# Three norms of a two-block transformer kernel: squares added over pairs of features by VectorE ahead of one ones product

## The reference, cut to what matters

```
def rmsnorm(x, g):
    x32 = x.astype(jnp.float32)
    y = x32 * lax.rsqrt(jnp.mean(x32 * x32, axis=-1, keepdims=True) + EPS)
    return (y * g.astype(jnp.float32)).astype(x.dtype)
```

## Time and profile before

| | us |
|---|---|
| median of 3 runs | 1694.67 |
| lowest, highest | 1693.54, 1696.02 |
| profiled execution | 1695.31 |
| its span, first to last instruction | 1693.1 |
| PE busy | 1655.0 (98%) |
| DVE busy | 1168.1 (69%) |
| ACT busy | 922.9 (55%) |
| POOL busy | 756.2 (45%) |

### The profile page before, as it was taken

One profiled execution on the slowest core, in us unless ns is written; L12 is line 12 of the kernel. 1 busy time (PEld: TensorE's weight loads), 2 busy tenths in 40 slices (PEclk: granted clock), 3 DMA queues, 4 the chain that ended last, 5 costly groups with the idle time before them and its releaser, 6 DMA issues.

```text
span 1693.1 us, 31046 instructions
## 1 busy us (share of the span) xinstructions
PE 1655.0 (98%) x10698; PEld 1467.9 (87%) x10698; DVE 1168.1 (69%) x2092; ACT 922.9 (55%) x1515; POOL 756.2 (45%) x357
## 2 busy tenths in 40 slices
PE   8999999999999999999999999999999999999998
PEld 8778999988999998888888879968899988789997
DVE  4772289777777777788777876365755579675555
ACT  4573455587666665545455464265555564555554
POOL 4500668888999991000000004403455744235553
PEclk9999999999999999999999999999999999999999
DMA  6303555587555547888888863303555543146553
GB/s 248 99 27 120 168 201 184 185 284 264 180 178 168 181 165 256 287 287 290 291 291 288 289 232 100 98 2 125 174 186 185 184 149 117 62 153 187 186 185 123
DMA packets 86343, 312.38 MB, mean 184 GB/s; under 512 B 9843, under 2 KB 9843, under 8 KB 86131
## 3 DMA queue, kind: packets, MB, share of 16 engines
q1 hardware_dynamic: 85972, 309.38, 54.5%
q0 software_dynamic: 288, 1.97, 0.3%
HBM read 310.26 MB, written 1.05 MB: 184 GB/s over the span
## 4 chain that ended last, share of the span: by engine, by line
PE 84%; DVE 7%; ACT 3%; issue 3%; POOL 1%; DMA 1%; DVEq 0%; SPq 0%; ACTq 0%; POOLq 0%
PE psr L898 17%; PE psr L838 15%; PE psr L1154 10%; PE acc_all L1154 10%; PE psr L901 9%; PE acc_all L838 7%; PE psr L1101 3%; PE psr L1046 2%; PE psr L785 1%; DVE arena L2561 1%; POOL wl L571 1%; DVE wl L571 1%; ACT wh L562 1%; PE psr L933 1%; PE psr L826 1%
## 5 line engine op out<-in xcount | busy, mean ns | idle before, releaser
L571 POOL TENSOR_TENSOR wl<-ring,wh 128x1024 fp32r<-128x1024 f32 x276 | 674.2, 2445 | 556.9 <-ACT wh L562 541.5
L562 ACT ACTIVATE wh<-ring 128x1024 fp32r<-128x1024 f32 x470 | 494.7, 1054 | 300.0 <-PE psr L838 150.5
L898 PE MATMUL psr<-hb,wh 128*128 128x512 f32 x1344 | 343.6, 397 | 0.7 <-DVE hb L1982 0.7
L571 DVE TENSOR_TENSOR wl<-ring,wh 128x1024 fp32r<-128x1024 f32 x194 | 240.4, 1239 | 61.2 <-ACT wh L562 60.1
L898 PEld LDWEIGHTS psr<-hb,wh 128*128 128x128 f32 x1344 | 240.8, 189 | 45.7 <-DVE hb L1982 2.3
L838 PE MATMUL psr<-hb,wh 128*128 128x256 f32 x1600 | 213.4, 286 | 6.4 <-DVE hb L1979 3.7
L838 PEld LDWEIGHTS psr<-hb,wh 128*128 128x128 f32 x1600 | 200.7, 192 | 10.5 <-DVE hb L1979 4.5
L901 PEld LDWEIGHTS psr<-hb,wl 128*128 128x128 f32 x1344 | 182.7, 190 | 15.9 <-DVE wl L571 1.7
L1154 PE MATMUL psr<-wh,hb 128*128 128x512 f32 x504 | 196.1, 389 | 0.0
L1154 PE MATMUL acc_all<-wh,hb 128*128 128x512 f32 x504 | 196.1, 389 | 0.0
L901 PE MATMUL psr<-hb,wl 128*128 128x256 f32 x1344 | 187.7, 282 | 1.0 <-DVE wl L571 0.8
(11 more groups left out here) (373 smaller groups left out, 2722.6 us busy)
## 6 DMA issues: line engine op xcount, KB each, us to landing
ring<-in_peer_u SPq DMA_DIRECT2D x128, 512.0 KB, 3.5
ring<-in_peer_v SPq DMA_DIRECT2D x128, 512.0 KB, 5.1
sq<-in_ada_w SPq DMA_DIRECT2D x91, 512.0 KB, 4.1
ring<-in_ffn_a SPq DMA_DIRECT2D x44, 512.0 KB, 4.0
ring<-in_ffn_b SPq DMA_DIRECT2D x44, 512.0 KB, 3.4
ring<-in_ffn_d SPq DMA_DIRECT2D x44, 512.0 KB, 3.5
ring<-in_pw SPq DMA_DIRECT2D x24, 512.0 KB, 3.6
ring<-in_w_in SPq DMA_DIRECT2D x18, 512.0 KB, 3.4
```

Source lines behind the costliest of these rows:

```text
L562: nc.scalar.activation(wh[:, q % 2, :], ring[:, s, :], ACT.Copy).then_inc(high_ready, 1)
L571: eng.tensor_tensor(wl[:, q % 2, :], ring[:, n % NS, :], wh[:, q % 2, :], ALU.subtract)\
L898: mm(ps[:, :], wh[:, b, chunk(k)], hb[:, k, :, :], start=(k == 0), stop=False, skip_group_check=True)
```

## The change

The squares of three norms are no longer multiplied with ones pair by pair. DVE adds the pairs of squares in place, 128x512 at a time: pair 1 onto pair 0 as part of raw lows 1, pair 2 as part of raw lows 2, pair 3 as part of raw lows 3, each counted by a new semaphore `folded`. In the woven tile PE leaves out the ones products of the first three quarters. In the last it waits for the third addition, makes the two ones products over the sum, and goes on as before. The waits for the squares move from PE to DVE.

```
+FOLDED = (5, 8, 11)
...
+        folded = sem("folded")
...
                 for k in range(KC):
-                    if sums is not None and k % 2 == 0:
+                    if sums in FOLDED and k % 2 == 0:
+                        if k == KC - 2:
+                            pe.wait_ge(folded, 3 * FOLDED.index(sums) + 3)
+                            for c in range(2):
+                                last = mm(ps[:, 0:T], ones, sq[:, c * T:(c + 1) * T], start=(c == 0), stop=(c == 1),
+                                          skip_group_check=True)
+                            fills(last, ("norm", sums))
+                        pe.wait_ge(raw_low, 4 * turn + k // 2 + 1)
+                    elif sums is not None and k % 2 == 0:
                         pe.wait_ge(squares, squares_before(sums) + k // 2 + 1)
...
-            def raw_lows(turn, gain, q):
-
+            def raw_lows(turn, gain, q, sums=None):
+
+                if sums is not None and q:
+                    dve.wait_ge(squares, squares_before(sums) + q + 1)
+                    if q > 1:
+                        dve.wait_ge(folded, 3 * FOLDED.index(sums) + q - 1)
+                    TT(sq[:, 0:2 * T], sq[:, 0:2 * T], sq[:, 2 * q * T:(2 * q + 2) * T], ALU.add).then_inc(folded, 1)
                 dve.wait_ge(raw_high, 4 * turn + q + 1)
...
                 if c:
-                    raw_lows(0, par("ffn_norm"), c - 1)
+                    raw_lows(0, par("ffn_norm"), c - 1, 5)
             raw_low_parts(TILE_NO["pq", 0])
-            raw_lows(0, par("ffn_norm"), 3)
+            raw_lows(0, par("ffn_norm"), 3, 5)
             raw_low_parts(TILE_NO["pq", 1])
```

More of the change, by code:

```diff
@@ L2439, in _ @@
                 if c:
-                    raw_lows(2, gsc[:, 2, :], c - 1)
+                    raw_lows(2, gsc[:, 2, :], c - 1, 8)
             raw_low_parts(TILE_NO["a", 0, 0])
-            raw_lows(2, gsc[:, 2, :], 3)
+            raw_lows(2, gsc[:, 2, :], 3, 8)
             raw_low_parts(TILE_NO["b", 0, 0])
@@ L2607, in _ @@
                 if c:
-                    raw_lows(4, gsc[:, 4, :], c - 1)
+                    raw_lows(4, gsc[:, 4, :], c - 1, 11)
             raw_low_parts(TILE_NO["a", 1, 0])
-            raw_lows(4, gsc[:, 4, :], 3)
+            raw_lows(4, gsc[:, 4, :], 3, 11)
             raw_low_parts(TILE_NO["b", 1, 0])
```

## The result

| | before | after |
|---|---|---|
| median, us | 1695.15 (17 runs) | 1697.47 (17 runs) |
| lowest, highest | 1693.35, 1697.49 | 1696.36, 1701.91 |
| mean, us | 1695.13 | 1698.48 |
| ratio, 95% interval | | 1.0023 (1.0016 to 1.0029) |
| profiled execution, its span | 1695.31, 1693.1 | 1700.77, 1698.9 |

The forecast was no change, 1695.3. The median lies in the stated range, but the kernel moved, by more than its interval, to the slower side. The ratio says 3.9 us, the means 3.35, the medians 2.3: the executions after spread to the upper side. Four executions of over 2000 us, three of the kernel before and one of e_only_5, are left out of all that follows.

What follows compares the result with a forecast made beforehand. PE was taken as the bound, with VectorE full too: 7.7 us of PE work become idle. Shifts of +0.18, +0.39 and -0.18 us, taken as +0.6 with slower restarts, bring 1694.67 to 1695.3 us; range 1692.6 to 1698.2.

Steps and rivals of the forecast that it cites:

- What goes: In norms 5, 8 and 11 PE loses three of four pairs of ones products: 2.58 us each, 7.7 us over three.
- Addition 1 hidden: Ahead of raw lows 1, addition 1 fits beside VectorE's waits; bounds 0 and 0.3 us, taken as 0.
- Additions 2 and 3 on a full VectorE: Ahead of raw lows 2 and 3, not hidden: 0.69 us each, next start 0.60 later, raw lows 3 1.20 later.
- PE's gaps: PE idles 1.2 to 1.6 us before chunk 4's raw products and about 1.1 to 1.2 before the ones products.
- The shift of the stages at whole clock: First tile's low products shift +0.18, +0.39, -0.18 us in norms 5, 8, 11: +0.39 to +1.11, taken as +0.6.
- That the raw lows decide: In the last quarter ones products end at D + 2.11, raw lows 3 at D + 2.08; PE goes on at D + 2.13.
- that the clock stays whole: In the three norms' new PE gaps the clock was to stay at 1.00; chance of any fall 0.16.
- Rival B: Clock falls in the new gaps, 1.7 us each, 5.1 for three, giving 1700.4; chance 0.16 any, 0.08 two or more.
- one fall or three: Cases of clock falls in the norms: one gives 1697.0, chance 0.08; all three 1700.4, two or more chance 0.08.
- a PE idle of 1.71 us at 1147: Idle at 1147.06 in the kernel before, with more behind it, cited against rival B because the clock stayed whole.
- Rival A: PE is the only bound and VectorE's additions fit in; 7.7 us gained, 1687.0; chance 0.05.
- Rival C: Additions cost more than their row, addition 1 beside GpSimd; price under 1 us, 1696.0; chance 0.05.

Runs made afterwards that it cites:

- e_only_5: The change in norm 5 alone, norms 8 and 11 as in the kernel before; median 1695.7 us, ratio 1.0009 to the kernel before.
- e_only_11: The change in norm 11 alone, norms 5 and 8 as in the kernel before; median 1696.2 us, ratio 1.0005 to the kernel before.
- after_again: The changed kernel measured once more, unaltered, in the third comparison on one chip; median 1697.9 us, ratio 1.0015 to the kernel before.
- e5_all_filled: The changed kernel with PE's new gaps in norms 5, 8 and 11 filled by small unused matmuls; median 1695.7 us, ratio 1.0009 to the kernel before.
- v_first_pair: Against the changed kernel, only addition 1 kept; PE makes ones products over that sum and pairs three and four; median 1692.4 us, ratio 0.9990 to the kernel before.
- e_no_additions: The changed kernel without VectorE's additions, the three norms summing chunks 0 and 1 only; median 1693.4 us, ratio 0.9989 to the kernel before.

## Why the prediction was wrong

The step that failed is the one on the clock; the sum of the stages held.

- **What goes: right.** 36 records of the ones line went.
- **Addition 1 hidden: right.** In norm 11 VectorE's next work starts 1.53 us after addition 1 begins (1489.83 behind 1488.30 in e_only_11), 1.50 before (1488.79 behind 1487.29).
- **Additions 2 and 3 on a full VectorE: right.** 0.69 us each, 0.60 to the next start, no idle bracket.
- **PE's gaps: right in place, nearly in size.** Forecast 1.3 and 1.2 in norm 5, measured 1.34 and 1.00. In norm 11 the first is 0.98, less than the 1.2 to 1.6 named for all three norms.
- **The shift of the stages at whole clock: right.** Norm 5 +0.32 (profile of the changed kernel), norm 8 +0.47 (after_again: 5.83 us from the end of the output products at 1175.16 to 1180.99), norm 11 -0.05 (e_only_11). Sum +0.74; the forecast took +0.6 within 0.39 to 1.11. That the raw lows decide held, too: in norm 5 raw lows 3 end at 167.04 and PE goes on at 167.09.
- **What failed: that the clock stays whole.** The forecast put the clock's cost at nothing. Rival B had the mechanism, the place and a price, and got a chance of 0.16 for any fall. The stages account for 0.7 us; the other 2.4 to 2.9 us of the mean are half clock. B's price of 1.7 us a fall was about right: norm 8's cost 2.08 - 0.47 = 1.6 us, norm 11's, twice as long in both profiles of the changed kernel (6.8 us), 2.0, as part of it lay in PE's waits. And as a fall comes in some executions and not in others, the mean was the thing to forecast, not "one fall or three".
  The rule of the Trainium skill (Perfetto Trace Analysis, Matmul Optimizations) was quoted and weighed too lightly: matmuls are to be executed back to back in batches, as PE scales its power with its use. The runs agree: with the gaps filled (e5_all_filled) the loss in the mean fell from over 3 us to 1.3.
- **Why the chance was too low.** The evidence against it was a PE idle of 1.71 us at 1147 "that left the clock whole". That was one draw. At the very same idle the clock fell in ten of the ten other profiles in which it was not filled. That filling it raised the mean clock of the kernel before (0.9963 to 0.9978) says that it had such falls as well, in executions that were not profiled.
- **Rival A is out:** nothing of the 7.7 us was had. The Trainium skill (Perfetto Trace Analysis, Optimizing Scalar/DVE Operations) suggests taking work off a saturated VectorE, and the stages agree, read by the stretch: VectorE was full there and each norm's raw lows came later. With one addition, where VectorE has room, v_first_pair has a gain: 0.79 us in norm 8's stage, 1.8 us in the mean.
- **Rival C:** no addition was longer than 693 ns; out.

Left open: how often each norm's fall comes, why one fall lasts 3.4 us and another 6.8, and where the slower executions of v_first_pair and e_no_additions lose their clock; one profile of each kernel is too few. Untested is whether any shortening of PE's work in these norms, without a long gap, lowers the clock as well; v_first_pair is the only kernel that bears on it, and its profile shows no fall there.

## What to carry to other kernels

Moving work off the bound engine pays only up to the point where the helper is late; behind it the saved work turns into gaps, and on PE gaps can cost more than the work that filled them: here 7.7 us of matmuls, turned into gaps of 0.9 to 1.5 us, left the kernel 3.1 to 3.6 us slower in the mean. Judge a move by the helper's free time in that stretch (here at least 0.6 us for the first addition, none for the others), and take as much as fits. A profile is one draw of the clock: compare the mean clock over all executions before a stretch is called safe.

## What was not expected of the hardware

- Time and clock go together over whole kernels: on one chip the mean granted clock fell from 0.9963 to 0.9944, 3.3 us in 1695, and the mean time rose by 3.1 us. But a fall behind PE's last instruction counts in that clock and costs nothing (0.9 us of it in the kernel before, 2.9 in v_first_pair).
- Two PE idles of 1.5 and 1.0 us, 0.6 us of work apart, brought half clock in norm 8 in one execution and not in another of the same program. It lasted 3.4 us there. Behind norm 11 it lasted 6.8 us in both, and began as PE came out of its first new gap (at 1495.6, PE starts at 1495.81).
- At half clock four ones records of 128x256 took 2.02 us, at whole clock 1.13 behind a gap.
- After a wait for a VectorE flag PE starts ones products 0.05 us later (addition ends at 166.25, start 166.30), and the quarter then takes 1.44 us, where 1.34 is the pace without a gap; in it PE also waits for raw lows 3.
